# A transformer pair of blocks on one core: the first 128 tokens go ahead from the end of the output projection

## What is computed

```python
mod = jax.nn.silu(c) @ w_ada + b_ada
shift1, scale1, gate1, shift2, scale2, gate2 = ...
...
x = x + gate1 * (y_mix @ w_out)
h2 = rms_norm(x, norm2_w) * (1.0 + scale2) + shift2
x = x + gate2 * peer_ffn(h2, peer_wq, peer_subkeys, peer_u, peer_v)

def peer_ffn(h, ...):
    q = (hb @ peer_wq).reshape(B, Q_BLOCK, PEER_HEADS, 2, PEER_HALF)
    s = jnp.einsum('bqhpd,hpnd->bqhpn', q, peer_subkeys)
    vals, idx = lax.top_k(s, PEER_TOPK)
    ...
    top_s, pos = lax.top_k(combo, PEER_TOPK)
    g = jax.nn.softmax(top_s, axis=-1)
    a = jax.nn.gelu(jnp.einsum('bqhkd,bqd->bqhk', peer_u[expert], hb))
    return jnp.einsum('bqhk,bqhkd->bqd', g * a, peer_v[expert])
```

## Time and profile before

| What | Value |
|---|---|
| median of 3 runs | 1338.79 us (1335.85 to 1339.43) |
| profiled execution, own time | 1342.23 us |
| its span | 1340.5 us |
| TensorE matmuls busy | 1115.8 us (83%) |
| VectorE busy | 828.4 us (62%) |
| ScalarE busy | 443.4 us (33%) |
| GpSimd busy | 404.0 us (30%) |
| moved by DMA | 384.87 MB, of it 268.45 MB by the gathers' queue |

### The profile page before, as it was taken

The page is one execution under the profiler, slowest core; times in us unless marked ns, Lnnn a source line. Parts: engine busy times, 40 slices in busy tenths (PEclk is TensorE's granted clock), DMA queues, the critical chain, the costliest instruction groups (busy, mean ns, idle before and its releaser), DMA issues.

```text
span 1340.5 us, 21867 instructions
## 1 busy us (share of the span) xinstructions
PE 1115.8 (83%) x8560; PEld 1071.4 (80%) x8560; DVE 828.4 (62%) x1790; ACT 443.4 (33%) x980; POOL 404.0 (30%) x376
## 2 busy tenths in 40 slices
PE   1889886889989887688778687789999698999876
PEld 1889875878888887678777677789989687998875
DVE  6689786666666766667766674554443735534363
ACT  4445632122221222221222221133733325462443
POOL 3463004233333433333333333250002712000350
PEclk7899888999999999989899998999999898997988
DMA  8864476999999999999999999954432514432230
GB/s 323 341 234 158 159 277 254 421 420 420 421 421 420 421 420 421 421 421 420 421 420 421 420 421 421 405 221 151 158 111 67 206 59 170 146 126 95 95 126 33
DMA packets 61402, 384.87 MB, mean 287 GB/s; under 512 B 6897, under 2 KB 9969, under 8 KB 19441
## 3 DMA queue, kind: packets, MB, share of 16 engines
q0 software_dynamic: 36864, 268.45, 48.2%
q1 hardware_dynamic: 22672, 112.76, 23.0%
q10 hardware_dynamic: 1762, 2.22, 0.5%
HBM read 382.36 MB, written 1.05 MB: 286 GB/s over the span
## 4 chain that ended last, share of the span: by engine, by line
PE 50%; DMA 32%; DVE 10%; issue 4%; ACT 3%; POOL 1%; SPq 0%; DVEq 0%; ACTq 0%; POOLq 0%
DMA low_pairs<-in_peer_uv,work 15%; DMA rows<-in_peer_uv,work 15%; PE aux L1191 12%; PE pj L1006 10%; PE pj L1007 9%; PE pj L1008 9%; PE aux L1170 3%; DMA rows<-in_w_ada 1%; DVE rows L1283 1%; DVE low_pairs L1519 1%; PE aux L1125 1%; DVE rows L1519 1%; PE aux L1104 1%; DVE wlo L516 1%; DVE xl L1581 1%
## 5 line engine op out<-in xcount | busy, mean ns | idle before, releaser
L1006 PE MATMUL pj<-xh,whi 128*128 128x256 f32 x1048 | 312.3, 298 | 68.2 <-DVE wlo L516 26.8
L1191 PE MATMUL aux<-work,rows 128*128 128x128 f32 x2368 | 290.6, 286 | 76.8 <-ACT work L880 75.8
L1191 PEld LDWEIGHTS aux<-work,rows 128*128 128x128 f32 x2368 | 283.4, 201 | 83.5 <-ACT work L880 82.3
L1007 PE MATMUL pj<-xl,whi 128*128 128x256 f32 x1048 | 306.1, 292 | 0.0
L1008 PE MATMUL pj<-xh,wlo 128*128 128x256 f32 x1048 | 305.6, 292 | 0.0
L1006 PEld LDWEIGHTS pj<-xh,whi 128*128 128x128 f32 x1048 | 210.8, 201 | 75.5 <-DVE wlo L516 24.1
L1191 PE MATMUL aux<-work,low_pairs 128*128 128x128 f32 x1728 | 210.8, 284 | 47.0 <-ACT work L880 47.0
L1191 PEld LDWEIGHTS aux<-work,low_pairs 128*128 128x128 f32 x1728 | 205.2, 200 | 52.3 <-ACT work L880 52.3
L666 POOL DMA_INDIRECT rows<-in_peer_uv,work x148 | 139.3, 941 | 311.4 <-PE aux L1191 225.3
L1007 PEld LDWEIGHTS pj<-xl,whi 128*128 128x128 f32 x1048 | 211.3, 202 | 0.3 <-issue 0.2
L1008 PEld LDWEIGHTS pj<-xh,wlo 128*128 128x128 f32 x1048 | 210.7, 201 | 0.0
(11 more groups left out here) (203 smaller groups left out, 1182.6 us busy)
## 6 DMA issues: line engine op xcount, KB each, us to landing
wring<-in_w SPq DMA_DIRECT2D x70, 1024.0 KB
rows<-in_w_ada SPq DMA_DIRECT2D x48, 512.0 KB, 6.2
wring<-in_w SPq DMA_DIRECT2D x20, 512.0 KB
rows<-in_peer_uv,work POOLq DMA_INDIRECT x148
low_pairs<-in_peer_uv,work POOLq DMA_INDIRECT x108
xT<-in_xT SPq DMA_DIRECT2D x1, 1024.0 KB, 7.7
wring<-in_w SPq DMA_DIRECT2D x4, 256.0 KB
work<-in_lnv ACTq DMA_DIRECT2D x1, 1024.0 KB
```

Of the source, the lines that this page charges most:

```text
L1006: mm(o, w[0], x[0], start=start, stop=False)
L1007: mm(o, w[0], x[1], start=False, stop=False)
L1191: ins = mm(peer_sum[t][:, c * P:(c + 1) * P], pair(n)[:, D + c * P:D + (c + 1) * P], diag[:, n % PICKS, :], start=(n % (EXPERT_HEADS * PIC ...
```

## The change

From the end of the output projection the two halves of the tokens are handled apart, the first 128 ahead. The sums of squares move between the pairs of chunks of the projection, in two sums of 128 columns. The last chunk's update, its square, the root, the reciprocal, the products and the shift are done by halves. TensorE multiplies the first half with head 0's queries and keys, then turns it, before ScalarE shifts the second half. Head 0's ordinary queries and scores are for the second half only. VectorE's routing of group 0 waits for the early scores alone; it keeps its place in VectorE's program.

```diff
-            for c in range(KC):
+            halves_ = [slice(t * P, (t + 1) * P) for t in range(NT)]
+            for c in range(KC - 1):
...
                     round_to(c + 34)
-            act.wait_ge(sums, 2)
-            nc.scalar.activation(rstd[:, :], aux[:, 5, 0:T], ACT.Sqrt, bias=eps[:, 0:1], scale=1.0 / D).then_inc(std_ready, 1)
-            for c in range(KC):
-                act.wait_ge(h_scaled, KC + c + 1)
-                nc.scalar.activation(hT[:, c, :], hT[:, c, :], ACT.Identity, bias=mod[:, 3 * KC + c:3 * KC + c + 1]).then_inc(h_ready, 1)
+            act.wait_ge(early_added, 1)
+            nc.scalar.activation(sq[:, KC - 1, 0:P], xT[:, KC - 1, 0:P], ACT.Square).then_inc(squares, 1)
+            act.wait_ge(taken_dve, KC)
+            nc.scalar.activation(sq[:, KC - 1, P:T], xT[:, KC - 1, P:T], ACT.Square).then_inc(squares, 1)
+            for t, ts in enumerate(halves_):
+                act.wait_ge(sums, 2 + t)
+                nc.scalar.activation(rstd[:, ts], aux[:, 2 + t, 0:P], ACT.Sqrt, bias=eps[:, 0:1], scale=1.0 / D).then_inc(std_ready, 1)
+            def shift(t):
+                for c in range(KC):
+                    act.wait_ge(h_scaled, (1 + t) * KC + c + 1)
+                    h = hT[:, c, halves_[t]]
+                    nc.scalar.activation(h, h, ACT.Identity, bias=mod[:, 3 * KC + c:3 * KC + c + 1]).then_inc(h_ready, 1)
             def score_query(h):
+                ts = slice(P if h == 0 else 0, T)
...
                         act.wait_ge(expert_scores, h - 1)
-                    nc.scalar.copy(pq[:, h % 2, s, :], aux[:, 4 + s, 0:T]).then_inc(queries_out, 1)
+                    nc.scalar.copy(pq[:, h % 2, s, ts], aux[:, 4 + s, ts]).then_inc(queries_out, 1)
             def score_out(h):
                 act.wait_ge(expert_scores, h + 1)
-                nc.scalar.copy(s_all[:, h::EXPERT_HEADS, :], aux[:, h % 2, :].rearrange("p (n k) -> p n k", n=NT)).then_inc(scores_out, 1)
+                first = 1 if h == 0 else 0
+                nc.scalar.copy(s_all[:, h + first * EXPERT_HEADS::EXPERT_HEADS, :],
+                               aux[:, h % 2, first * 2 * KEYS:].rearrange("p (n k) -> p n k", k=2 * KEYS)).then_inc(scores_out, 1)
+            shift(0)
+            for s in range(2):
+                act.wait_ge(early_query, s + 1)
+                nc.scalar.copy(pq[:, 0, s, 0:P], aux[:, 4 + s, 0:P]).then_inc(early_query_out, 1)
+            act.wait_ge(early_scores, 1)
+            nc.scalar.copy(s_all[:, 0, :], aux[:, 0, 0:2 * KEYS]).then_inc(early_scores_out, 1)
+            shift(1)
             def gate_exps(g):
...
             turn_y(att1, ytok)
-            whole(input_parts(mix_split, lambda k: max(k + 1 + NT - HC, NT)), KC)
-            for c in range(KC):
-                pe.wait_ge(squares, KC + c + 1)
-                ins = mm(aux[:, 5, 0:T], ones[:, :], sq[:, c, :], start=(c == 0), stop=(c == KC - 1))
-            ins.then_inc(sums, 1)
-            pe.wait_ge(h_ready, 2 * KC)
+            mixed_in = input_parts(mix_split, lambda k: max(k + 1 + NT - HC, NT))
+            for c in range(0, KC + 2, 2):
+                if c < KC:
+                    whole(mixed_in, 2)
+                for k in range(max(c - 2, 0), c):
+                    for t in range(NT):
+                        pe.wait_ge(squares, KC + k + 1 if k < KC - 1 else 2 * KC + t)
+                        ins = mm(aux[:, 2 + t, 0:P], ones[:, :], sq[:, k, t * P:(t + 1) * P], start=(k == 0), stop=(k == KC - 1))
+                        if k == KC - 1:
+                            ins.then_inc(sums, 1)
             def turn_h2(t):
...
                 w = w_slot(n)
+                ts = slice(P if h == 0 else 0, T)
...
                     for k in range(KC):
-                        ins = mm(aux[:, 4 + s, 0:T], w[:, k, s * P:(s + 1) * P], hT[:, k, :], start=(k == 0), stop=(k == KC - 1))
+                        ins = mm(aux[:, 4 + s, ts], w[:, k, s * P:(s + 1) * P], hT[:, k, ts], start=(k == 0), stop=(k == KC - 1))
...
             def score_keys(h):
...
                     pe.wait_ge(scores_out, h - 1)
-                for t in range(NT):
+                for t in range(1 if h == 0 else 0, NT):
...
+            def early_scores_of_head_0():
+                w_wait(pe, UNITS_1.index(queries_of(0)))
+                w = w_slot(UNITS_1.index(queries_of(0)))
+                for s in range(2):
+                    for k in range(KC):
+                        if s == 0:
+                            pe.wait_ge(h_ready, KC + k + 1)
+                        ins = mm(aux[:, 4 + s, 0:P], w[:, k, s * P:(s + 1) * P], hT[:, k, 0:P], start=(k == 0), stop=(k == KC - 1))
+                    ins.then_inc(early_query, 1)
+                n = UNITS_1.index(keys_of(0))
+                w_wait(pe, n)
+                for s in range(2):
+                    pe.wait_ge(early_query_out, s + 1)
+                    ins = mm(aux[:, 0, s * KEYS:(s + 1) * KEYS], pq[:, 0, s, 0:P], w_slot(n)[:, 0, s * KEYS:(s + 1) * KEYS], start=True, stop=True)
+                ins.then_inc(early_scores, 1)
+            early_scores_of_head_0()
+            pe.wait_ge(taken_dve, KC)
+            turn_h2(0)
+            pe.wait_ge(h_ready, 3 * KC)
             score_query(0)
+            pe.wait_ge(early_scores_out, 1)
             score_keys(0)
-            turn_h2(0)
...
             def part(n):
...
-            def norm(n, weight, scale):
-                chain.link(v.tensor_scalar(gain[:, :], part(scale), 1.0, None, ALU.add))
-                chain.link(v.tensor_tensor(gain[:, :], gain[:, :], cols[:, weight:weight + KC], ALU.mult))
-                dve.wait_ge(std_ready, n + 1)
-                chain.link(v.reciprocal(rstd[:, :], rstd[:, :]))
-                for c in range(KC):
-                    v.scalar_tensor_tensor(hT[:, c, :], xT[:, c, :], gain[:, c:c + 1], rstd[:, :], ALU.mult, ALU.mult).then_inc(h_scaled, 1)
+            def second_norm():
+                chain.link(v.tensor_scalar(gain[:, :], part(4), 1.0, None, ALU.add))
+                chain.link(v.tensor_tensor(gain[:, :], gain[:, :], cols[:, N2W:N2W + KC], ALU.mult))
+                for t in range(NT):
+                    ts = slice(t * P, (t + 1) * P)
+                    dve.wait_ge(std_ready, 2 + t)
+                    chain.link(v.reciprocal(rstd[:, ts], rstd[:, ts]))
+                    for c in range(KC):
+                        v.scalar_tensor_tensor(hT[:, c, ts], xT[:, c, ts], gain[:, c:c + 1], rstd[:, ts], ALU.mult, ALU.mult).then_inc(h_scaled, 1)
...
                 chunk_wait(dve, m)
-                v.scalar_tensor_tensor(xT[:, c, :], chunk_out(m), mod[:, 2 * KC + c:2 * KC + c + 1], xT[:, c, :], ALU.mult, ALU.add) \
-                    .then_inc(taken_dve, 1)
-                ada_dots(late + c, late + c + 1)
+                if c < KC - 1:
+                    v.scalar_tensor_tensor(xT[:, c, :], chunk_out(m), mod[:, 2 * KC + c:2 * KC + c + 1], xT[:, c, :], ALU.mult, ALU.add) \
+                        .then_inc(taken_dve, 1)
+                    ada_dots(late + c, late + c + 1)
+                else:
+                    for t in range(NT):
+                        ts = slice(t * P, (t + 1) * P)
+                        v.scalar_tensor_tensor(xT[:, c, ts], chunk_out(m)[:, ts], mod[:, 2 * KC + c:2 * KC + c + 1], xT[:, c, ts], ALU.mult, ALU.add) \
+                            .then_inc(taken_dve if t else early_added, 1)
+            ada_dots(late + KC - 1, late + KC)
             ada_bias(3 * KC, 5 * KC)
+            dve.wait_ge(early_added, 1)
             dve.wait_ge(taken_dve, KC)
-            norm(1, N2W, 4)
+            second_norm()
...
             def flat2(ap):
...
             def route_halves(g):
-                dve.wait_ge(scores_out, min(g, EXPERT_HEADS - 1) + 1)
+                if g == 0:
+                    dve.wait_ge(early_scores_out, 1)
+                else:
+                    dve.wait_ge(scores_out, min(g, EXPERT_HEADS - 1) + 1)
...
             def route_pairs(g):
```

More of the change, by code:

```diff
@@ L373, in build @@
         queries, queries_out = sem("queries"), sem("queries_out")
+        early_added, early_query, early_query_out, early_scores, early_scores_out = (
+            sem("early_added"), sem("early_query"), sem("early_query_out"), sem("early_scores"), sem("early_scores_out"))
         expert_scores, scores_out = sem("expert_scores"), sem("scores_out")
```

## The result

The changed kernel took 1341.97 us (median of 20 runs, 1339.51 to 1344.81); the kernel before, run beside it, 1339.62 (20 runs, 1333.37 to 1340.95). The ratio is 1.0022, with a 95% interval of 1.0013 to 1.0032: **slower by 0.2%**, inside 0.3% of no change, but clear of zero. By means it is +3.2 us, by medians +2.4. The profiled execution took 1341.72 us (span 1340.0). The profiled execution of before (1342.23) lies above all 20 of its timed runs, so the two profiles can't be subtracted as totals. They can be compared stage by stage, each from the start of the output projection (160.19 us before, 160.16 after).

The account below looks back on a forecast made before the run. DMA was taken to bound the kernel from 220 to 870 us, its end set by when it saturates. A later first gather was covered by weight loads shifting -1.05 to +0.95: net 0 +- 1.0 us, so 1338.8 us, range 1335.0 to 1342.0.

Parts of the forecast that it names:

- the saturated stretch: Expert-row gathers, 220 to 870 us: DMA 1.01 busy at 420 GB/s, ending when a fixed number of bytes has moved.
- the moment of full DMA: When DMA becomes saturated for good, after the projection; the only earlier thing said to move the stretch's end; forecast 213.6 to 215.6.
- second theory of the expectations: From the experiments' forecasts: something other than the moment DMA becomes full for good sets the end.
- The sums do not hide: Output projection on TensorE: 16 sum matmuls hide under nothing, so the projection ends 1.8 us later.
- the first gather: First load of expert rows, behind VectorE's routing; forecast issued at 216.4 instead of 215.16, covered by weight loads.
- Rival A: Faster: early scores let routing and the first gather start early, DMA saturating 6.1 us earlier; 1332.7 us, chance 0.05.
- Rival C: Sums hide in the projection, which ends no later, so every start is 1.8 us earlier; 1337.0 us, chance 0.10.
- the clock: TensorE before head 0's queries: head 1's 1.05 us earlier if the clock stays high, 0.95 later if it falls; middle taken.
- rival B: Slower: TensorE's clock stays at 1.2 GHz across the wait for second shifts, DMA starting +3.0 us; 1341.8 us, chance 0.12.

Follow-up runs that it names:

- e12: Kernel before with five unread reciprocals on VectorE ahead of the routing, holding back only the gathers; ratio to before 1.0028, +3.4 us by means.
- e10: Kernel before with 28 unread matmuls in TensorE's wait ahead of head 0's queries; ratio to before 0.9973, -3.6 us by means.
- e3: Changed kernel with ScalarE's second-half shifts moved ahead of the early query and score copies; ratio to before 1.0010, +0.0 us by means.
- e4: Changed kernel with VectorE's w_ada dots moved ahead by two, none behind the last two chunks; ratio to before 0.9997, -0.4 us by means.
- e6: Changed kernel run again unaltered on another chip; ratio to before 1.0020, +3.2 us by means.
- e7: Changed kernel with w_ada dots moved ahead by two and second-half shifts before the early copies; ratio to before 0.9987, -1.9 us by means.
- e5: Kernel before run again unaltered on another chip; ratio to before 0.9996, -0.5 us by means.
- e9: Changed kernel with unread matmuls on TensorE, 12 before the early queries and 8 before the second half; ratio to before 0.9985, -1.5 us by means.
- e1: Kernel before with only the norm sums, 256 columns in one piece, moved between pairs of projection chunks; ratio to before 1.0018, +2.9 us.

## Why the prediction missed

**What held.** That the end of the saturated stretch hangs on the moment of full DMA is shown: over 13 profiles, in which that moment moves between 51.6 and 57.7 us from the start of the projection, the last dot follows it 652.1 to 654.4 us later. A count by bytes needs no reading of single seconds: take 240 us less what DMA moved from its first filled second up to there, at 420 GB/s. By it the moment lies between 52.8 and 58.9 us, and the last dot 651.5 to 653.0 us behind it in all 14 profiles, e12 with its hole included. The timed differences by means follow the table's moments with about 1 us of scatter (1.9 at most, e10). The second theory of the expectations falls. What sets the moment is shown as well: head 1's queries start at 43.6 to 49.8 us in the kernels without fill, and DMA is full 0.7 to 1.0 us after they end. The sums do not hide: 22.50 of 22.50 us busy, the update 1.5 us later (forecast 1.8; the projection of the changed kernel ran three fewer of its first matmuls at the low clock, with a pitch of 0.213 instead of 0.120 us, which makes up the 0.3). The norm started at 191.09 (191.4), a halved reciprocal took 0.95 us as forecast, the two updates 0.60 us. The w_ada dots started at 197.27 (197.5). Routing waited for nothing and started at 207.17 (208.1), the first gather at 215.46 (216.4): both 0.9 us sooner, of which 0.2 came from the start of the dots. The rest is in the dots, which took 9.9 instead of 10.54 us, nearly all of it a shorter wait for one w_ada tile (0.33 instead of 0.91 us). Rival A did not come, for the reason given: the dots stand ahead. Rival C fell with the projection's end.

**The step that failed** is *the clock*: "I take the middle, no difference". The clock fell in every unfilled profile with early queries (changed, e3, e4, e6, e7), around waits of 2.2 to 2.8 us, so there was no middle to take. And the loss was sized a little too small: "if it does, 2.0 - 1.05 = 0.95 later" took the 2.0 us of the earlier trace rows, where the two halves lost 2.3 and 2.6 us. That makes 1.25 and 1.55 us; head 1's queries in fact started 1.2 us later than before in the first pair of profiles and 1.7 in the second (e6 against e5), outside the upper end of 0.95, and DMA was full 1.4 and 1.8 us later. The delay runs through the path that the prediction named: the early scores came at 200.8 instead of 198.8, and the second half's shifts behind their copy came 1.9 us later too. The other end of the step is what e9 shows, with the clock held: forecast 1.05 us earlier, measured 1.6 us for head 1's queries and 1.5 +- 1.2 us less time. So the step gives +1.4 to +1.8 of a measured +3.2 by means (+2.4 by medians, interval of the ratio from 1.7 us up); the rest is open, see below.

**Why rival B's number is no hit for rival B.** Its 1341.8 is near 1341.97, but its mechanism didn't happen: it needed head 1's queries to end after 216.6 (they ended at 215.05), and DMA to start with the gather at 217.6 (216.0, with the weight units, ahead of the first gather's data). Where the clock did fall across the second wait, in e6, the second half took 1.6 us more (5.47 against 3.84), not the 3.6 of the rival, and both halves together lost only 0.3 us more, since the clock came back sooner in the first. The measured 1341.97 also lies inside the range of 1335.0 to 1342.0, by 0.03 us and at the end that only rival B had put there; that is luck. (By its own sum the lower end would be 1337.0 - 1.05 - 1.5 = 1334.45.)

**How much is the clock?** Kept high, before gains 3.6 +- 1.4 us (e10) and the changed kernel 4.7 +- 1.7 (e9 against the changed kernel, each by its difference to before). So both kernels lose to it, and what it takes more from the changed one, 1.1 us, is not clear of zero. Between the filled two 2.1 +- 1.5 us are left, with no clock in them. They are work that was added to the path and bought little: the sums lengthen the projection (1.8 us in e1), what they uncover is filled by two dots (e4), and the early part returns little because the second shifts stand behind its copies (e3). Both obstacles taken away turn +3.2 into -1.9 (e7).

**What stays open.** The profiles show DMA full 1.4 and 1.8 us later (1.4 and 1.3 by bytes), and the last dot of the saturated stretch only 0.9 us later in both pairs, counted from the projection's start, where the timed means show +3.2; e10 gains 3.6 by means and 1.7 in its profile. A profile is one execution, and the projection's own start varies by 2.2 us between them (159.6 to 161.8), the stretch behind the last dot by 6 (466.2 to 472.2 us to the end of the span). Whether the remainder is such scatter or a second small loss was not settled.

## What to carry to other kernels

Work moved from behind a producer that is busy throughout into it costs its full length there; ask what the shortened tail was hiding, and whether the part that is to profit stands first in the order of every engine it passes (here ScalarE's early copies and two of VectorE's dots stood in its way). Where an engine's clock falls after short waits, splitting one block into two with a wait before each can lose more than it overlaps; price it at the low clock, not halfway. A few unread matmuls across a wait are a test that costs two lines, and here the test on the kernel before beat the change.

## What the hardware did that I had not expected

TensorE's granted clock fell to 1.2 GHz (0.50) after waits of different length. In the changed kernel TensorE was busy 0.72 and 0.56 of 188 to 190 and last worked at 190.2; the clock was at 0.93 in 191 to 192 and at 0.50 from 192 on, so it fell 1.7 us behind the last work. Before, it was busy without a gap until 189.08, and the clock fell 3.4 us behind that. Around the same wait of 1.93 us the clock stayed high once, and in e4 and e6 it fell 1.3 and 0.9 us after work had begun again. It came back 2.9 us after work had begun at the earliest (e6) and 6.2 us at the latest (e1), where the prediction counted on 4; that spread alone moves head 1 by over a microsecond from one execution to the next. Unread matmuls of ones held it at 1.00 throughout (e9, e10) and did not slow what came behind them: head 1's queries took 7.07 us as everywhere.
